# Norm columns in PSUM, weight residuals ahead of activation residuals on GpSimd, and a projection block in two halves

## What is computed

```
def rms_norm(u, g):
    y = uf * lax.rsqrt(jnp.mean(uf * uf, axis=-1, keepdims=True) + NORM_EPS)
    return (y * g.astype(F32)).astype(u.dtype)
...
        hl = rms_norm(xl, norm_g[i, 0]) * (1 + sc_a) + sh_a
...
            yl, yc = ab_mixer(hl, hc, row, col, lp, need_ctx)
        else:
...
            yl = conv_mixer(hl, conv_w_in[o], conv_w[o], conv_w_out[o])
...
        xl = xl + gt_a * rms_norm(yl, norm_g[i, 1])
        hm = rms_norm(xl, norm_g[i, 2]) * (1 + sc_m) + sh_m
        xl = xl + gt_m * rms_norm(sq_relu_mlp(hm, mlp_w1[i], mlp_w2[i]), norm_g[i, 3])
```

## Time and profile before

| | |
|---|---|
| median of 3 runs | 1702.07 us (1699.81 to 1708.38) |
| the profiled execution | 1700.18 us, of it span 1698.4 us |
| PE, PEld busy | 1575.9 us (93%), 1293.3 us (76%) |
| DVE, ACT, POOL busy | 714.8 us (42%), 565.9 us (33%), 865.9 us (51%) |
| granted TensorE clock, mean | 0.967 of full speed |
| weights and other reads | 157.71 MB, 94 GB/s over the span |
| where norms 1, 2, 3 lie | 728 to 760, 1099 to 1134, 1310 to 1342 us |

### The profile page before, as it was taken

One profiled execution on the slowest core, in us unless ns is written; L12 is line 12 of the kernel. 1 busy time (PEld: TensorE's weight loads), 2 busy tenths in 40 slices (PEclk: granted clock), 3 DMA queues, 4 the chain that ended last, 5 costly groups with the idle time before them and its releaser, 6 DMA issues. The chain is left out here.

```text
span 1698.4 us, 35413 instructions
## 1 busy us (share of the span) xinstructions
PE 1575.9 (93%) x15544; PEld 1293.3 (76%) x15544; DVE 714.8 (42%) x1112; ACT 565.9 (33%) x810; POOL 865.9 (51%) x404
## 2 busy tenths in 40 slices
PE   5899999988888888989999999999989899999996
PEld 3688868767676776858888888888868688888885
DVE  1343246667677754662121212750385611212135
ACT  3423246543435223243132323232223422223230
POOL 1432205098869652438888888744432444444441
PEclk9999899998999999989999999979989899999998
DMA  7322001022313122224444344222221222222221
GB/s 321 129 75 73 12 1 50 1 102 78 127 45 111 55 102 83 75 74 150 149 148 141 136 145 147 99 74 98 84 90 51 74 99 100 100 99 93 89 90 50
DMA packets 23617, 162.15 MB, mean 95 GB/s; under 512 B 2624, under 2 KB 3264, under 8 KB 4800
## 3 DMA queue, kind: packets, MB, share of 16 engines
q1 hardware_dynamic: 21904, 154.09, 25.2%
q10 hardware_dynamic: 1584, 6.13, 0.9%
HBM read 157.71 MB, written 2.10 MB: 94 GB/s over the span
## 5 line engine op out<-in xcount | busy, mean ns | idle before, releaser
L215 POOL TENSOR_TENSOR v<-raw,v 128x1024 fp32r<-128x1024 f32 x160 | 388.9, 2453 | 388.3 <-ACT v L209 388.3
L232 PE MATMUL bank<-hm,v 128*128 128x512 f32 x1968 | 447.9, 389 | 1.4 <-PEq L1937 1.4
L232 PEld LDWEIGHTS bank<-hm,v 128*128 128x128 f32 x1968 | 369.1, 188 | 79.2 <-issue 2.6
L232 PE MATMUL bank<-hid,v 128*128 128x512 f32 x1536 | 349.5, 389 | 0.0
L232 PEld LDWEIGHTS bank<-hid,v 128*128 128x128 f32 x1536 | 288.3, 188 | 59.9
L209 ACT ACTIVATE v<-raw 128x2048 fp32r<-128x2048 f32 x80 | 153.2, 1915 | 411.9 <-PE bank L232 411.8
L2262 DVE TENSOR_TENSOR bank<-bank,rl 128x512 f32<-128x512 f32 x64 | 44.8, 700 | 263.7 <-ACT rl L2234 263.7
L1041 POOL TENSOR_TENSOR raw<-raw,cs 128x2048 f32<-128x2048 f32 x24 | 86.7, 3612 | 100.4 <-issue 64.3
L215 POOL TENSOR_TENSOR w<-raw,w 128x1024 fp32r<-128x1024 f32 x22 | 54.1, 2482 | 136.2 <-ACT w L209 136.2
L534 PE MATMUL bank<-h,w 128*128 128x512 f32 x600 | 109.7, 345 | 0.0
L534 PEld LDWEIGHTS bank<-h,w 128*128 128x128 f32 x600 | 93.7, 191 | 15.3 <-issue 1.1
(11 more groups left out here) (362 smaller groups left out, 2339.2 us busy)
## 6 DMA issues: line engine op xcount, KB each, us to landing
raw<-w_in SPq DMA_DIRECT2D x119, 1024.0 KB, 4.8
mraw<-wm_in SPq DMA_DIRECT2D x16, 1024.0 KB, 4.8
raw<-wm_in SPq DMA_DIRECT2D x3, 1024.0 KB, 16.2
xres<-x_in ACTq DMA_DIRECT2D x1, 2048.0 KB, 8.2
yb<-wm_in SPq DMA_DIRECT2D x2, 1024.0 KB, 19.4
mixed_in<-wm_in SPq DMA_DIRECT2D x2, 1024.0 KB, 23.2
xres<-x_in SPq DMA_DIRECT2D x1, 2048.0 KB, 7.6
out_T<-xres ACTq DMA_DIRECT2D x8, 256.0 KB, 2.0
```

Of the source, the lines that this page charges most:

```text
L215: i = nc.gpsimd.tensor_tensor(W[1][n % 2][:, k:k + 4], raw[n % 2][:, k:k + 4], W[0][n % 2][:, k:k + 4].bitcast(F32), SUB)
L232: last = nc.tensor.matmul(bank(b(s, m), 0, hi - lo), W[w][s][:, k, m * P:(m + 1) * P], H[h][:, k, lo:hi], start=(k == 0 and w == h == 0), ...
```

## The change

- **First stage.** ACT rounds block 1 in two halves (L339 to 343 of the new text), POOL makes the remainder of the first half only. The second half's remainder is the first thing on POOL's list in the second stage. `second_block` takes the place of `pe_block` for block 1 on PE: it starts on the first half and waits for the second ahead of channel tile 4.
- **Norms, the small steps.** What was written to `rcol[:, 1, :]` by steps 2 and 3 goes to PSUM (bank 4, columns 8 to 12); the fourth and fifth step read it there. Each of the last four steps now has a PSUM input.
- **Norms, PE's order.** The cross sum comes ahead of the first spread. Between the spreads stand 4 late columns in place of 6 (norm 2), or two 128x128 matmuls in place of one 128x512 (norms 1 and 3).
- **Norms, DVE's order.** The five steps come first, then `update(0)`, then the second reciprocal, and only then `update(1)` and `residual(0)`.
- **Norms, POOL.** Both weight blocks are split first, then the remainders of tiles 1, 3, 4 and 5; tile 4 was DVE's. There is a third `nhf` buffer, and ACT's work for tile 4 becomes two instructions.

```
@@ first stage, ACT and POOL
-                act_hi(act, S_IN + 1, W)
+                s = (S_IN + 1) % 2
+                act.wait_ge(raw_loaded[s], 16)
+                for j, done in enumerate((half_hi, hi_ready[s])):
+                    k = slice(4 * j, 4 * j + 4)
+                    nc.scalar.activation(W[0][s][:, k], raw[s][:, k], ACT.Copy).then_inc(done, 1)
...
-                pool_lo(pool, S_IN + 1, W)
+                s = (S_IN + 1) % 2
+                pool.wait_ge(half_hi, 1)
+                nc.gpsimd.tensor_tensor(W[1][s][:, 0:4], raw[s][:, 0:4], W[0][s][:, 0:4].bitcast(F32), SUB)\
+                    .then_inc(half_lo, 1)
@@ second stage, PE and POOL
+                def second_block():
+
+                    s = (S_IN + 1) % 2
+                    pe.wait_ge(half_lo, 1)
+                    for m in range(2):
+                        for k in range(KT):
+                            if m == 0 and k == KT // 2:
+                                pe.wait_ge(split_ready[s], 1)
+                            for w, e in ((0, 0), (0, 1), (1, 0)):
+                                last = nc.tensor.matmul(bank(2 * (2 * s + m)), W[w][s][:, k, m * P:(m + 1) * P],
+                                                        hT[e][:, k, C:N], start=k == w == e == 0,
+                                                        stop=(k == KT - 1 and w == 1))
+                        last.then_inc(tile_done[s][m], 1)
...
+                s = (S_IN + 1) % 2
+                pool.wait_ge(hi_ready[s], 1)
+                nc.gpsimd.tensor_tensor(W[1][s][:, 4:8], raw[s][:, 4:8], W[0][s][:, 4:8].bitcast(F32), SUB)\
+                    .then_inc(split_ready[s], 1)
@@ norms
-            hf = [sb(st, f"nhf{i}", [P, T]) for i in range(2)]
+            hf = [sb(st, f"nhf{i}", [P, T]) for i in range(3)]
...
-            by_pool = (1, 3, 5)
+            by_pool = (1, 3, 4, 5)
@@ norms, PE
+                    pe.wait_ge(sums.made, sums.done(last, "product"))
+                    token_sums(pe, sums.sums[1], cross_sum, True, True).then_inc(cross_done, 1)
                     pe.wait_ge(inv_ready, 1)
                     over_partitions(pe, rcol[:, 0, :], rms_y).then_inc(spread_done, 1)
-                    pe.wait_ge(sums.made, sums.done(last, "product"))
-                    token_sums(pe, sums.sums[1], cross_sum, True, True).then_inc(cross_done, 1)
-                    late_columns(0, 6)
+                    late_columns(0, 4)
                     if late is None:
-                        keep_warm(1, bank(5))
+                        keep_warm(2, bank(5), P)
                     pe.wait_ge(inv_ready, 2)
                     over_partitions(pe, rcol[:, 1, :], rms_x).then_inc(spread_done, 1)
-                    late_columns(6, 20)
+                    late_columns(4, 20)
@@ norms, DVE
+                    dve.wait_ge(inv_ready, 1)
+                    dve.wait_ge(cross_done, 1)
+                    part, turn = rcol[:, 1, :], bank(4, 2 * TG, 3 * TG)
+                    link(nc.vector.tensor_tensor(part, scaled_sum, r, MUL))
+                    link(nc.vector.scalar_tensor_tensor(turn, cross_sum, 2.0, part, MUL, ADD))
+                    link(nc.vector.tensor_tensor(turn, turn, r, MUL))
+                    link(nc.vector.tensor_tensor(turn, turn, v, ADD))
+                    link(nc.vector.tensor_scalar(v, turn, 0.0, None, MAX))
                     dve.wait_ge(spread_done, 1)
                     update(0)
...
+                    dve.wait_ge(root_ready, 2)
+                    nc.vector.reciprocal(rcol[:, 1, :], rcol[:, 1, :]).then_inc(inv_ready, 1)
                     update(1)
                     residual(0)
-                    dve.wait_ge(root_ready, 2)
-                    nc.vector.reciprocal(rcol[:, 1, :], rcol[:, 1, :]).then_inc(inv_ready, 1)
@@ norms, POOL
                     pool_lo(pool, n0, W)
-                    remainder(1)
                     pool_lo(pool, n0 + 1, W)
-                    remainder(3)
-                    remainder(5)
+                    for k in by_pool:
+                        remainder(k)
```

More of the change, by code:

```diff
@@ L273, in build @@
                  "rst_done", "hf_ready", "hs_ready", "hhi_ready", "h_even", "h_odd", "dve_chain")
+        half_hi, half_lo = sems(until_rwkv, "half_hi", "half_lo")
         (const_in, x_in, cst_in, csig, cs_ready, eps_ready, early_used, rows_ready, folded, mod_ready, sq_ready, sq_used,
@@ L567, in spread @@
                     last.then_inc(kspread, 1)
+                def second_block():
[10 more added lines that the diff above has]
+                        last.then_inc(tile_done[s][m], 1)
                 for n in range(S_IN + 1, S_MOD):
-                    if n < S_IN + 4:
+                    if n == S_IN + 1:
+                        second_block()
+                    elif n < S_IN + 4:
                         pe_block(pe, n, W, hT, parts=both[:1])
@@ L1924, in norms @@
             rms_y, rms_x = bank(6), bank(7)
-            by_pool = (1, 3, 5)
+            by_pool = (1, 3, 4, 5)
+            by_vector = tuple(k for k in range(KT) if k not in by_pool)
             def scratch(k):
-                return hf[k // 2 % 2][:] if k in by_pool else bank(other) if k == last else bank(4)
+                return hf[by_pool.index(k) % 3][:] if k in by_pool else bank(other) if k == last else bank(4)
             def shift(k):
@@ L1933, in h_done @@
             def h_done(k):
-                return (h_odd, k // 2 + 1) if k in by_pool else (h_even, min(k // 2 + 1 + (k == last), 5))
+                if k in by_pool:
+                    return h_odd, by_pool.index(k) + 1
+                return h_even, by_vector.index(k) + 1
             with nc.Block() as block:
@@ L1965, in _ @@
                             nc.scalar.activation(f, f, ACT.Identity, bias=shift(k), scale=1.0).then_inc(hs_ready, 1)
-                            act.wait_ge(hs_ready, k // 2 + 1)
+                            act.wait_ge(hs_ready, by_pool.index(k) + 1)
                             i = nc.scalar.activation(h[0][:, k], f, ACT.Copy)
@@ L2040, in scaled @@
                         dve.wait_ge(x_ready, k + 1)
-                        if k in (2, 4, 6):
-                            dve.wait_ge(h_even, k // 2)
-                        if k == 5:
-                            dve.wait_ge(h_odd, 1)
+                        if k in by_vector[1:-1]:
+                            dve.wait_ge(h_even, by_vector.index(k))
+                        if k in by_pool[3:]:
+                            dve.wait_ge(h_odd, by_pool.index(k) - 2)
                         nc.vector.scalar_tensor_tensor(scratch(k), x[:, k, :], nsc[:, 3, k:k + 1], rms_x, MUL,
@@ L2054, in _ @@
                     r, v = rcol[:, 0, :], power
+                    dve.wait_ge(inv_ready, 1)
[6 more added lines that the diff above has]
+                    link(nc.vector.tensor_scalar(v, turn, 0.0, None, MAX))
                     dve.wait_ge(spread_done, 1)
                     update(0)
-                    dve.wait_ge(inv_ready, 1)
-                    dve.wait_ge(cross_done, 1)
-                    turn = rcol[:, 1, :]
-                    link(nc.vector.tensor_tensor(turn, scaled_sum, r, MUL))
-                    link(nc.vector.scalar_tensor_tensor(turn, cross_sum, 2.0, turn, MUL, ADD))
-                    link(nc.vector.tensor_tensor(turn, turn, r, MUL))
-                    link(nc.vector.tensor_tensor(v, v, turn, ADD))
-                    link(nc.vector.tensor_scalar(v, v, 0.0, None, MAX))
+                    dve.wait_ge(root_ready, 2)
+                    nc.vector.reciprocal(rcol[:, 1, :], rcol[:, 1, :]).then_inc(inv_ready, 1)
                     update(1)
                     residual(0)
-                    dve.wait_ge(root_ready, 2)
-                    nc.vector.reciprocal(rcol[:, 1, :], rcol[:, 1, :]).then_inc(inv_ready, 1)
                     for k in range(KT):
```

## The result

The changed kernel takes 1693.47 us (median of 6 runs, 1689.95 to 1696.08), the kernel before 1703.47 us beside it (6 runs, 1699.81 to 1708.38). The ratio is 0.9928 [0.9912, 0.9944]: faster by 10.0 us, where 11.1 were forecast. The range was 1686 to 1698. In a second session the ratio was 0.9917 [0.9888, 0.9946] (1692.08 us, 6 runs, against 1706.06, 11 runs).

What follows compares the result with a forecast made beforehand. PE, busy 93% of the span, was taken as the bound, with time only in its pauses or lower clock. First stage 3.6, norm 1 3.4, norm 2 1.3 and norm 3 2.8 make 11.1 us: 1691.0 us, range 1686 to 1698.

Steps and rivals of the forecast that it cites:

- The first stage: End of the first stage: POOL's half-size remainder saves 2.35 us and the kept clock 1.25, together 3.6 us.
- The clock: Behind the first stage's end: PE's shorter pause keeps the clock up, worth 1.25 us more (bounds 0 to 1.25).
- The small steps: Norms: a DVE step with two SBUF inputs waits for POOL's running instruction; the five steps now take 0.20 us each.
- No price for PSUM: Norms' small steps: reading PSUM costs nothing extra; by the skill's rule, some 0.2 us in each norm.
- The reciprocal beside POOL: Norms: the reciprocal, with one SBUF input, runs while POOL works at no cost; up to 1.4 us if it waits.
- S: Start of a norm's first scaled tile (L2045): 2.8 us earlier in norm 3, 3.4 in norm 1 (4.3 or 2.4).
- The tail neither gains nor loses: Norms 1 and 3, from S to block end: S + 18.9 against S + 18.86; bounds -1 and +1.5 us each.
- Norm 2: PE is the bound from its second spread on; PE's pause ahead of that spread goes, gaining 1.3 us.
- the tail eats the head: Rival, chance 0.16: POOL's four remainders make PE wait, losing the gain at S in norms 1 and 3; 1697 us.
- the clock stays down: Rival, chance 0.04: narrower matmuls between spreads keep the clock down through norms 1 and 3's 48 matmuls; 1712 us.
- it does not reach the end: Rival, chance 0.05: earlier stages finish earlier but later ones wait for loads or POOL; 1701 to 1702 us.
- More than forecast: Rival, chance 0.09: the clock stays up in norms 1 and 3, some 3 us more together; 1688 us.

## Why the prediction was right

- **The first stage** (3.6 forecast, 3.87 measured). POOL's half: 2.35 against 2.3 measured. The clock: 1.25, taken from the upper end of its bounds, against 1.57. PE's pause came out at 1.02 where 0.95 stood. That the clock would stay up was argued from a pause of 1.38 us inside norm 3, and the run with useless matmuls shows that it is the pause that lets it fall. The clock's share is larger since the yardstick was too long: the 7.41 us for 30 matmuls at full speed came from norm 3, where the same count took longer than it does here. In the changed kernel the first 30 of block 1 took

```profile
64.82 7.09 PE L586 MATMUL bank<-h,w 128*128 128x512 f32 x30 [1.02 <-PEq L283]
```

  and 8.66 - 7.09 is the 1.57 measured. (The pause ahead of the 30 matmuls in norm 3 was the one of 1.27, not of 1.38 us; that changes nothing.)
- **The small steps** (the mechanism of norms 1 and 3). Right, and shown by the run that put two of them back into SBUF: one step then takes 2.05, the next 2.26, and the norms lose 7.2 us.
- **No price for PSUM.** By an estimate from the Trainium skill (VectorE: DVE Perf Modes, The TRN2 errata) the three changed steps were to cost some 0.2 us a norm. In norm 3 they took 0.17 each, start to start 0.20 to 0.21, and those of before 0.16 where nothing held them up. A hundredth of a microsecond each, so the row was the better guide here.
- **The reciprocal beside POOL**, costed at nothing with up to 1.4 us as its bound: 0.17 us, in norms 1 and 3.
- **S.** Norm 3: 2.8 forecast, 2.66 measured (12.84 - 10.18). Norm 1: 3.4 and 3.59. Here the forecast had luck. Before, POOL's end set S, so it stood at 12.6 to 12.9 in norms 1 and 3 of all three kernels with the old steps, however fast PE was. Now PE's chain sets it, and S in norm 1 lies between 8.6 and 11.0 by the clock. My bounds for norm 1 were 4.3 if the spread stays at the full clock and 2.4 if the reciprocal waits. The second has nothing to do with the clock, and a slow start falls below it: with S at 10.87 or 11.00 norm 1 gains only 1.8 or 1.6 us. The sum took a middle value, and the traced execution happened to have it.
- **The tail neither gains nor loses**: 19.32 against 19.32 and 19.33. Also the places: 1.35, 0.90 and 0.28 at tiles 2, 4 and 5, where "about 1", 1.0 and 0.4 stood. One step of it was incomplete: the end before was put down to the late tile 3 (S + 11.45), and the one after to tiles 4 and 5, as if two different limits happened to agree. It was tile 5 in both, at S + 14.42, with tile 3 of the kernel before just out of the way (by an estimate two tiles of 1.48 us from S + 11.45 are done at S + 14.4). So the wait of 1.3 us at tile 3, one of the two long ones in the row, was worth nothing, and hid the small one that counted.
- **Norm 2** (1.3 forecast, 0.74 measured) is the term that was mis-sized. The step "PE runs through" was right; PE's timeline of the changed kernel has no pause ahead of the second spread or of the late columns:

```profile
1105.32 2.05 PE L188 MATMUL bank<-cst,nrcol 128*128 128x128 f32 x8
1107.16 6.83 PE L2009 MATMUL bank<-cst,late 128*128 128x1 f32 x32
1113.85 2.91 PE L2042 MATMUL bank<-hm,v 128*128 128x512 f32 x6
...
1117.27 2.36 PE L2042 MATMUL bank<-hm,v 128*128 128x512 f32 x6
...
1119.83 1.63 PE L2042 MATMUL bank<-hm,v 128*128 128x512 f32 x6
```

  Tile 0 started 17.76 us after the norm's start, where it was 18.97: 1.21 us earlier, nearly the forecast. But from tile 0 to the norm's end it took 16.78 us in place of 16.31. PE's time there isn't constant: tile 1 took 2.36 us, while the clock returned from the lower level, tile 2 took 1.63. When the clock falls and returns moves norm 2 between 32.9 and 34.6 in the kernels with all of the new norms, a gain of 0.7 to 2.4; a single number for it had no footing in one profile.

Of the rivals, "the tail eats the head" is refuted by the tails, "the clock stays down" by the windows and tails (in norm 3 the clock was back ahead of S, in norm 2 it returned at tile 1; in norm 1 it fell once more behind S, and tiles 0 to 3 took 7.57 us without a pause, where in norm 3 they took 7.52 with the wait of 1.35 in it: the slow matmuls filled that wait, and the tail stayed at 19.32), and "it does not reach the end" by the medians. "More than forecast" is half true: in some executions the clock did stay up longer in a norm, but in others it fell at once, so it is a spread of 1.6 to 2.4 us in each norm and no gain to count on. The window of norm 1 in question, in the changed kernel (columns as above):

```profile
743.00:747.00 4.00, 4.00 (x12) 2.53 (x11) 4.00 (x8) 2.04 (x3) 1.06 (x2) 0.57 0.77 266
```


What stays open: why the clock falls more in the attention stages of some executions, what the waits there in others are, and what decides when the clock falls in a norm. No run was made for these. Nor was DVE's new order, or the narrower work between the two spreads on PE, taken back by itself.

## What to carry to other kernels

A tiny VectorE step can cost as much as a whole GpSimd instruction if it reads two tensors from SBUF while GpSimd works: look in the timeline for small steps whose ends agree with GpSimd's, and give them a PSUM input, or move them. A long wait in a chain of tiles need not set its end: here four placements gave one and the same end, since a later tile's way through VectorE set it, and only taking work off VectorE ahead of that tile shortened it. And compare the segments that the change touches, in more than one execution, since an untouched stretch can move by as much as the gain.

## What was not expected of the hardware

- A VectorE step with one SBUF input, too, was slow beside GpSimd. In the second stage L714 (`TENSOR_SCALAR`, 128x8, SBUF to SBUF) ran beside POOL's moved half (L635, 64.81 to 67.23) and took 0.81 us, while the reciprocal of 128x4, also with one SBUF input, took 0.17 beside POOL. It ends at 67.25, with POOL's instruction. In all ten traced kernels with the moved half it took 0.81 to 0.83 us; in the three without it, where POOL is idle at this place, 0.11. So one SBUF input is no guarantee, and which steps wait is not settled by these runs. DVE's timeline of the changed kernel:

```profile
66.44 0.81 DVE L714 TENSOR_SCALAR small<-prm 128x8 f32<-128x8 f32 x1
```

- The granted clock needn't fall at the same point for the same instructions, and the earlier it falls, the later S comes: S in norm 1 was 8.60, 8.65, 9.00, 9.03, 9.04, 9.29, 10.87 and 11.00 us in executions whose PE and DVE lists are the same up to there.
- One-column matmuls kept PE busy for 3.87 of 4.00 us while the clock stayed at 0.50 (1104 to 1108 in the run with late columns behind the tiles). There it returned some 7 us after tile 0's start, in the eight executions with fewer of them between the tiles 3.2 to 6.0 us after it.
